# Layer 0's modulation in a two-layer transformer kernel: a third of it on TensorE, two thirds as row products on VectorE

## The reference, cut to what matters

```python
cond_x = jax.nn.silu(c);  cond_c = jax.nn.silu(c_ctx)
for i in range(DEPTH):
    mx = jnp.split((cond_x @ mod_w[i] + mod_b[i])[:, None, :], 6, axis=-1)
    mc = jnp.split(cond_c @ mod_w[i] + mod_b[i], 6, axis=-1)
    hx = x * (1.0 + mx[1]) + mx[0];  hc = ctx * (1.0 + mc[1]) + mc[0]
    yx, yc = mixer(hx, hc)                 # layer 0: HGRN2 with 8 heads, layer 1: window attention
    x = layer_norm(ALPHA * x + mx[2] * yx, ...)
    tokens = x * (1.0 + mx[4]) + mx[3]     # ctx likewise in layer 0
    x = layer_norm(ALPHA * x + mx[5] * peer_ffn(tokens, ...), ...)
```

## Time and profile before

| what | us |
|---|---|
| median of 3 runs (lowest, highest) | 3223.73 (3221.99, 3224.60) |
| the profiled execution: its own time | 3223.5 |
| its span, first to last instruction | 3221.7 |
| TensorE busy in the span | 2920.9 |
| VectorE busy | 2096.4 |
| ScalarE busy | 1157.4 |
| GpSimd busy | 638.0 |

### The profile page before, as it was taken

One profiled execution on the slowest core, in us unless ns is written; L12 is line 12 of the kernel. 1 busy time (PEld: TensorE's weight loads), 2 busy tenths in 40 slices (PEclk: granted clock), 3 DMA queues, 4 the chain that ended last, 5 costly groups with the idle time before them and its releaser, 6 DMA issues.

```text
span 3221.7 us, 43391 instructions
## 1 busy us (share of the span) xinstructions
PE 2920.9 (91%) x15541; PEld 2422.6 (75%) x15541; DVE 2096.4 (65%) x3641; ACT 1157.4 (36%) x1915; POOL 638.0 (20%) x423
## 2 busy tenths in 40 slices
PE   7799996798688999999999999688798789999997
PEld 1488884482377899999999999665597679999997
DVE  0166663479995677777777777845398655656666
ACT  0233330221274333333333333215246544444443
POOL 0000000230343233333333333200464100000000
PEclk9899997899899999999999999899899999999999
DMA  6311102324478888787788878520345766665654
GB/s 260 154 66 65 65 26 79 131 79 157 160 210 275 290 275 280 272 281 274 271 279 274 282 270 283 207 104 27 131 163 174 235 232 211 211 211 209 212 205 147
DMA packets 223271, 623.16 MB, mean 193 GB/s; under 512 B 16296, under 2 KB 104528, under 8 KB 216912
## 3 DMA queue, kind: packets, MB, share of 16 engines
q1 hardware_dynamic: 186332, 487.99, 43.2%
q0 software_dynamic: 36864, 134.23, 12.5%
HBM read 570.68 MB, written 51.48 MB: 193 GB/s over the span
## 4 chain that ended last, share of the span: by engine, by line
PE 78%; DVE 12%; DMA 4%; ACT 2%; POOL 2%; issue 2%; SPq 0%; DVEq 0%; POOLq 0%; ACTq 0%
PE bank L960 28%; PE bank L1005 26%; PE bank L776 5%; PE bank L995 3%; PE bank L883 3%; PE bank L917 2%; PE bank L830 2%; PE bank L741 2%; POOL arena L1934 2%; DVE arena L1727 1%; DMA arena<-in_wst 1%; PE bank L789 1%; DMA arena<-in_u 1%; PE bank L1043 1%; PE bank L1097 1%
## 5 line engine op out<-in xcount | busy, mean ns | idle before, releaser
L960 PE MATMUL bank<-h_parts,u_hi 128*128 128x384 f32 (+1 forms) x3904 | 869.0, 313 | 24.8 <-DVE u_lo L1732 19.9
L1005 PE MATMUL bank<-v_parts,p_hi 128*128 128x512 f32 x2560 | 799.5, 393 | 15.8 <-DVE p_lo L1753 15.4
L960 PEld LDWEIGHTS bank<-h_parts,u_hi 128*128 128x128 f32 x3904 | 676.0, 192 | 44.8 <-issue 17.3
L960 PE MATMUL bank<-h_parts,u_lo 128*128 128x384 f32 (+1 forms) x1952 | 610.4, 313 | 0.0
L1005 PEld LDWEIGHTS bank<-v_parts,p_hi 128*128 128x128 f32 x2560 | 473.2, 189 | 110.7 <-DVE p_lo L1753 14.2
L1005 PE MATMUL bank<-v_parts,p_lo 128*128 128x512 f32 x1280 | 502.4, 393 | 0.0
L1749 DVE TENSOR_TENSOR arena<-arena 128x384 f32<-128x384 f32 (+1 forms) x256 | 190.6, 744 | 418.2 <-ACT arena L1353 392.2
L1353 ACT ACTIVATE arena<-bank 128x384 f32<-128x384 f32 (+1 forms) x232 | 102.8, 443 | 878.1 <-PE bank L960 878.1
L960 PEld LDWEIGHTS bank<-h_parts,u_lo 128*128 128x128 f32 x1952 | 373.8, 192 | 0.0
L1751 DVE TENSOR_TENSOR v_parts<-arena,v_parts 128x1024 fp32r<-128x1024 f32 x256 | 313.7, 1225 | 56.1 <-ACT v_parts L1356 49.3
L1732 DVE TENSOR_TENSOR u_lo<-arena,u_hi 128x1024 fp32r<-128x1024 f32 x230 | 281.2, 1223 | 102.4 <-ACT u_hi L1254 97.8
(11 more groups left out here) (257 smaller groups left out, 3683.5 us busy)
## 6 DMA issues: line engine op xcount, KB each, us to landing
arena<-in_u SPq DMA_DIRECT2D x256, 512.0 KB, 3.6
arena<-in_v SPq DMA_DIRECT2D x256, 512.0 KB, 3.6
arena<-in_wst SPq DMA_DIRECT2D x39, 2048.0 KB, 7.6
gate_scratch<-arena SPq DMA_DIRECT2D x18, 2048.0 KB, 8.7
arena<-gate_scratch SPq DMA_DIRECT2D x32, 768.0 KB
arena<-in_whd SPq DMA_DIRECT2D x8, 2560.0 KB, 9.1
arena<-gate_scratch SPq DMA_DIRECT2D x32, 512.0 KB
x_scratch<-arena SPq DMA_DIRECT2D x10, 512.0 KB, 3.2
```

What stands on the lines that cost most here:

```text
L960: last = mm(banks[q][:, 0:ND[p]], w[:, q, col], h[:, k, DS[p]], start=(n3 == 0), stop=(n3 == 3 * KT - 1))
L1005: last = mm(banks[2 + 2 * b + half][:, :], x[:, q, b * P:(b + 1) * P], y[:, q, col], start=(first and i == 0), stop=(final and i == 2))
```

## The change

1. **Opening.** Only the first four tiles of layer 0's matrix (pieces 0 and 1) go through TensorE. They have four buffers of their own (`mod_at`), so that SP issues all four loads, those of `x` and `ctx` and that of the first head's weights without waiting for a use; each tile's rows are turned right after the next tile's products. The bias is turned into columns and copied to `modcol` first, and the columns of the products are added to it. `x` and `ctx` are loaded into slot `W[1]`; so the second head's weights are loaded once `x` is turned. ScalarE makes the first high parts (`high_w`) behind `modulate_x` and no longer ahead of it, and VectorE the low parts of pieces 0 and 1 behind its low parts of the tokens.
2. **Heads.** The other two thirds of the matrix come transposed (`wm`: 32 blocks of 128x1024, 512 KB, four per head, into two buffers that lie in the area of `hT`). The two conditions go through DRAM and are spread over all partitions (`cb`). For each block and stream VectorE forms the product with the condition and its sum over 1024 elements (`mod_sum`, a `tensor_tensor_reduce`): eight per head, one ahead of level 0, three right after level 0's copy, and one after each of the levels 1, 3, 5 and 7. At a head's end the eight sums are added to `modcol`.
3. **After the heads.** TensorE turns those columns back into rows (two transposes), ScalarE copies them, SP stores them in `modd` with two DMAs, waits for these, and only then issues the loads of the first norm.
4. **Expert loop of layer 0.** Group 1 is written out, and each of its eight steps issues one of the eight loads of the second norm (`ln_row`) behind the step's tile of `v`.
5. The per-slot semaphores of the query weights (`qw_h`, `qw_l`, `qw_pe`) become one each, with waits for the same events. `h_tok` takes scales to which 1 has been added already.

```diff
@@ SP, opening
-            with sp.Fori(0, MOD_TILES // 2) as n:
-                for s in range(2):
-                    sp.wait_ge(mod_pe[s], 1 + n)
-                    sp.dma_start(ar(W[s], KT * WCOLS), a["wst"][2 * n + s]).then_inc(w_loaded[s], 16)
...
-            sp.dma_start(modd[:, 0:MODN], modsb[:, :]).then_inc(mod_out, 16)
+            for i in range(FIRST):
+                sp.dma_start(ar(mod_at[i], KT * WCOLS), a["wst"][i]).then_inc(mod_in[i], 16)
+                if i == 0:
+                    sp.dma_start(lvlraw, a["lvlmask"]).then_inc(lvlmask_in, 16)
             for b in range(2):
                 sp.dma_start(xtok[:, b, :], a["ctx"][0, b * P:b * P + P, :]).then_inc(x_in, 16)
                 sp.dma_start(xtok[:, 2 + b, :], a["x"][0, b * P:b * P + P, :]).then_inc(x_in, 16)
+            sp.dma_start(ar(W[0], WSLOT), a["whd"][0]).then_inc(w_loaded[0], 16)
+            sp.wait_ge(setup_v, 3)
+            sp.dma_start(cs.rearrange("s (k d) -> (s k) d", d=P), condrow).then_inc(cs_out, 16)
+            sp.wait_ge(cs_out, 16)
+            sp.wait_ge(setup_t, 2)
+            sp.wait_ge(xT_pe, KT)
+            sp.dma_start(ar(W[1], WSLOT), a["whd"][1]).then_inc(w_loaded[1], 16)
+            sp.wait_ge(hT_l, KT)
+            for s in range(2):
+                sp.dma_start(cb[:, s, :], cs[s, :].partition_broadcast(P)).then_inc(cb_in, 16)
+            def mod_rows(h, s, x):
+                sp.wait_ge(wm_b, BLOCKS_M * h + (x + 1))
+                sp.dma_start(wm[:, x % 2, :], a["wm"][BLOCKS_M * h + x]).then_inc(wm_in[x % 2], 16)
+            with sp.Fori(0, HEADS // 2 - 1) as n:
                 for s in range(2):
+                    for x in range(BLOCKS_M):
+                        mod_rows(2 * n + s, s, x)
+                        if x == 1:
+                            sp.wait_ge(vproj, 4 * n + (2 * s + 1))
+                            sp.dma_start(ar(W[s], WSLOT), a["whd"][2 * n + (s + 2)]).then_inc(w_loaded[s], 16)
@@ SP, expert loop
+                def experts_and_row(j, q, N):
+                    experts(j, q, N)
+                    ln_row((j - 2) % 8)
...
                 if p == 0:
                     sp.wait_ge(mod1_out, 32)
-                ln_rows(p, 1, STREAMS[p], LN_BASE[p], BLOCKS[p], lambda b: xs[b])
-                with sp.Fori(max(nB, 1), GROUPS - 1) as n:
+                    group(1, experts_and_row)
+                else:
+                    ln_rows(p, 1, STREAMS[p], LN_BASE[p], BLOCKS[p], lambda b: xs[b])
+                with sp.Fori(max(nB, 2), GROUPS - 1) as n:
@@ SP, after the heads
-            sp.wait_ge(mod_out, 16)
+            sp.wait_ge(modT_a, 1)
+            for s in range(2):
+                rows = modd[s, 2 * D:CHUNKS * D].rearrange("(x d) -> x d", d=P)
+                sp.dma_start(rows, modT[:, s, :]).then_inc(mod_out, 16)
+            sp.wait_ge(mod_out, 32)
             ln_rows(0, 0, [0, 1], 0, range(4), x_of)
@@ TensorE
+            def mod_turn(i):
+                pe.wait_ge(mod_v, i + 1)
+                for x in range(4 * i, 4 * i + 4):
+                    last = nc.tensor.transpose(banks[6][:, 2 * x:2 * x + 2], modrow[:, x * P:(x + 1) * P], ident[0:2, 0:2])
+                last.then_inc(mod_t, 1)
+            for i in range(FIRST):
+                pe.wait_ge(mod_in[i], 16)
...
+                for k in range(KT):
+                    last = mm(banks[i % 2][0:2, :], cond[:, :, k], w[:, k, :], start=(k == 0), stop=(k == KT - 1))
+                last.then_inc(mod_pe, 1)
+                if i:
+                    mod_turn(i - 1)
+            mod_turn(FIRST - 1)
@@ ScalarE
-            act.wait_ge(w_loaded[0], 16 * (MT + 1))
+            modulate_x(0)
+            act.wait_ge(w_loaded[0], 16)
             for c in range(2):
                 high_w(0, c)
-            modulate_x(0)
@@ VectorE
+            def mod_sum(h, x, s):
+                col = sums[:, 2 * x + s:2 * x + s + 1]
+                if s == 0:
+                    dve.wait_ge(wm_in[x % 2], 32 * h + (16 * (x // 2) + 16))
+                    dve.wait_ge(wm_b, BLOCKS_M * h + (x + 2))
+                else:
+                    dve.wait_ge(wm_a, BLOCKS_M * h + (x + 1))
+                V.tensor_tensor_reduce(wm_out, wm[:, x % 2, :], cb[:, s, :], 1.0, 0.0, ALU.mult, ALU.add, col).then_inc(wm_b if s else wm_a, 1)
@@ VectorE, levels
                 if more:
                     low_w(h + 1, 1 - slot, 1)
+                mod_sum(h, 0, 0)
...
                     if l == 0:
                         V.tensor_copy(at, src).then_inc(lvlcp, 1)
+                        mod_sum(h, 0, 1)
+                        mod_sum(h, 1, 0)
+                        mod_sum(h, 1, 1)
                         continue
...
                         low_w(h + 1, 1 - slot, l // 2 + 1)
+                    if l % 2:
+                        mod_sum(h, 2 + l // 4, (l // 2) % 2)
@@ VectorE, head's end
                 finish(h, slot)
+                dve.wait_ge(wm_b, BLOCKS_M * h + (2 + BLOCKS_M))
+                m = modcol[:, 0, bass.ds(8 * h + 32, 8)]
+                link(V.tensor_tensor(m, sums, m, ALU.add))
...
-            for c in range(2, 5):
+            for c in range(5):
                 low_w(0, 0, c)
             low_w(1, 1, 0)
+            dve.wait_ge(cb_in, 32)
             scale_head(0, 0)
```

More of the change, by code:

```diff
@@ L178, in build @@
         setup_v = sem("setup_vector")
-        mod_pe = [sem(f"mod_product{i}") for i in range(2)]
-        mod_v = [sem(f"mod_biased{i}") for i in range(2)]
+        mod_in = [sem(f"mod_weights_loaded{i}") for i in range(4)]
+        mod_pe = sem("mod_products")
+        mod_v = sem("mod_rows_copied")
+        cs_out = sem("condition_stored")
+        cb_in = sem("condition_spread")
+        wm_in = [sem(f"mod_rows_loaded{i}") for i in range(2)]
+        wm_a = sem("mod_first_sums")
+        wm_b = sem("mod_sums")
+        modT_a = sem("mod_rows_turned")
         mod_out = sem("mod_stored")
@@ L230, in build @@
         keys_in = sem("keys_loaded")
-        qw_h = [sem(f"query_weights_high{i}") for i in range(4)]
-        qw_l = [sem(f"query_weights_low{i}") for i in range(4)]
-        qw_pe = [sem(f"query_products{i}") for i in range(4)]
+        qw_h = sem("query_weights_high")
+        qw_l = sem("query_weights_low")
+        qw_pe = sem("query_products")
         pq_sb = sem("queries_copied")
@@ L359, in wh @@
             return ar(W[slot], WSLOT, k=KT, n=HCOLS)
-        ORDER = ([("loop", i) for i in range(MOD_TILES)] + [("head", i) for i in range(HEADS)]
+        ORDER = ([("head", i) for i in range(HEADS)]
                  + [("wout0", i) for i in range(2)] + [("wq0", i) for i in range(4)] + [("mod1", i) for i in range(MOD_TILES)]
@@ L734, in _ @@
             nc.tensor.transpose(banks[3][:, 0:24], lbraw, ident[0:24, 0:24]).then_inc(setup_t, 1)
+            pe.wait_ge(bias_in, 16)
+            nc.tensor.transpose(banks[4][:, 0:96], biasraw, ident[0:96, 0:96]).then_inc(setup_t, 1)
             pe.wait_ge(setup_v, 1)
-            with pe.Fori(0, MOD_TILES // 2) as n:
-                for s in range(2):
-                    pe.wait_ge(w_loaded[s], 16 * n + 16)
-                    pe.wait_ge(mod_v[s], 1 + n)
-                    for k in range(KT):
-                        last = mm(banks[s][0:2, :], cond[:, :, k], wt(s)[:, k, :], start=(k == 0), stop=(k == KT - 1))
-                    last.then_inc(mod_pe[s], 1)
+            def mod_turn(i):
[5 more added lines that the diff above has]
+                pe.wait_ge(mod_in[i], 16)
+                w = ar(mod_at[i], KT * WCOLS, k=KT, n=WCOLS)
+                if i >= 2:
+                    pe.wait_ge(mod_v, i - 1)
+                for k in range(KT):
[4 more added lines that the diff above has]
+            mod_turn(FIRST - 1)
             def mod_columns(rows, n, bank):
@@ L747, in mod_columns @@
                 last.then_inc(mod_t, 1)
-            for s in range(2):
-                pe.wait_ge(mod_v[s], 1 + MOD_TILES // 2)
-            mod_columns(modsb, CHUNKS * KT, banks[6])
             def transpose_x(layer, need, src):
@@ L885, in mixer_out @@
                     last.then_inc(y_pe, 1)
+            pe.wait_ge(mod_c, 2)
+            for s in range(2):
+                last = nc.tensor.transpose(banks[7][0:32, s * P:(s + 1) * P], modcol[:, 0, 32 + s:96:2], ident)
+            last.then_inc(mod_t, 1)
             for h in range(HEADS):
@@ L891, in _ @@
             pe.wait_ge(onorm, HEADS)
+            pe.wait_ge(modT_a, 1)
             mixer_out("wout0", oT, WOUT_ORDER[0])
@@ L918, in query_unit @@
                             n3 += 1
-                    last.then_inc(qw_pe[m], 1)
+                    last.then_inc(qw_pe, 1)
                 def key_scores(i):
@@ L1445, in _ @@
             V.tensor_copy(lvlmask.rearrange("p l t -> p (l t)"), lvlraw)
-            dve.wait_ge(bias_in, 32)
-            with dve.Fori(0, MOD_TILES // 2) as n:
-                for s in range(2):
-                    dve.wait_ge(mod_pe[s], 1 + n + 1)
```

(9 more changed lines are left out.)

106 lines of the change are left out of this document (64 added, 42 removed).

## The result

Over four runs each, the changed kernel takes 3139.6 us (median; 3138.6 to 3141.6), the kernel before in the same session 3224.2 (3222.0 to 3224.7). The ratio is 0.974, with a 95% interval of 0.9723 to 0.9757: faster. The forecast was 3144.0, its range 3138 to 3159.

The account below looks back on a forecast made before the run. TensorE was taken to carry the chain in heads and expert loop, its products alternating with loads in the opening. Terms -73.2 + 0.7 + 2.7 - 9.7 = -79.5 took 3223.5 to 3144.0 us; range 3138 to 3159.

Parts of the forecast that it names:

- Opening: Before the first head: fewer tiles on TensorE and earlier tokens start projections at 62.3 against 135.53, minus 73.2 us.
- Clock: TensorE before the projections: idle some 4 us after the change as well, so priced at nothing; up to 1.8 us possible.
- Heads: Seven heads covering a next projection: eight sums each fit VectorE's idle gaps, 0.1 us per head, plus 0.7 us.
- R2: Rival in the heads: waits between sums exceed the gaps, 1 us in each of seven heads, 3150.3 us; chance 0.06.
- Last head: Last head, without a projection: three sums of 3.75 us meet 1.07 idle between levels 0 and 1, plus 2.7 us.
- A sum at 1.25: VectorE's sums in the heads: 1.25 us counted for each, with a wait on the sum before.
- R3: Rival in the heads: a sum costs double, 2.3 us, and misses the gaps, giving 3192 us; chance 0.05.
- Row blocks: Loads in the heads: a third block takes 5.2 us in all against 6 us of room, cost nothing.
- R4: Rival in the heads: row blocks queue behind head weights; a landing of 17 gives 3232 us, slower than before; chance 0.02.
- After the heads: Before the first norm: turning, copying and stores delay its loads 4 to 5 us, covered by 25 us, cost nothing.
- Expert loop: Layer 0's expert loop: spread row loads remove 10.2 us of waiting and slow products, 0.5 given back, minus 9.7 us.
- R1: Rival in the expert loop: the stall spreads over eight steps, most of the 10.2 us returns, 3152 us; chance 0.12.

Follow-up runs that it names:

- e4: The kernel after, with each of the 64 sums computed twice, one behind the other: 3207.2 us.
- e2: The kernel before, with only the second norm's eight row loads spread over the second group of experts, one per expert: 3213.4 us against 3222.5.
- e9: The kernel before, with GpSimd's two low parts of layer 0's first u tiles held back until VectorE has written the last block's choices: 3224.5 us against 3222.4.
- the shifted loop: The kernel after, with 45 small VectorE instructions more ahead of its loop over pairs of heads, the loop itself unchanged: 3138.1 us.
- e3: The kernel after, with each of the 64 sums cut from 1024 to 8 elements, so the modulation sums are left out: 3136.2 us.
- e6: The kernel after, with the last head's eight sums placed one before level 0 and one behind each level from 1 to 7: 3137.1 us.
- e1: The kernel after, with the second norm's eight row loads of layer 0 put back in one batch behind the first group of experts: 3149.4 us.

## Why the prediction was right

**Opening: forecast minus 73.2, measured minus 77.2.** The mechanism held at each step: TensorE sets the end, the fourth tile waits for nothing, the 12.50 us for `x` are gone. Mis-sized was the way to the first `modulate_x`, forecast at 47.3, measured at 43.32. 1.9 us of that are the first tile: I took 13.5 and its products began at 11.63. Half of it is its issue, which moved ahead too (3.62, against 4.56) and which I left out; the other half is its landing in 7.87 us instead of 10.21, 2.3 less where I had taken off 1.4 for the masks. Another 1.9 are products and turns, 29.8 us from 11.63 to 41.47 against 31.7. The slow start gives 1.2 of them: the first two tiles took 15.24 us, not the 9.39 + 7.04 of the earlier trace rows. The turns give 0.5, since two of 0.34 stand between the tiles where I had counted three of 0.4; the third runs beside the last copy. The 1.2 are luck of the execution: the same 32 products take 15.24 us here and 15.53 to 16.72 in the nine experiments with this opening. Their first `modulate_x` stands at 43.40 to 44.61, up to 1.3 us later, but the copy of the first head's level 0 at most 0.8 later (e4 apart, whose sum before it is doubled). From the first `modulate_x` to the projections it is 15.05 us, 15.0 forecast.

**Clock: priced at nothing, and nothing came** ahead of the projections (0.50 in 50 to 60 us). But late in the kernel it made a difference: layer 1's first 16 products took 5.41 us, 3.72 before. Windows of these 10 us, the kernel before, then after:

```profile
2107.00:2117.00 10.00, 8.82 (x38) 7.16 (x39) 3.34 (x9) 0.95 (x3) 0.00 (x0) 1.00 0.00 0
```

```profile
2021.00:2031.00 10.00, 9.30 (x34) 7.47 (x34) 2.77 (x7) 0.56 (x2) 0.00 (x0) 0.83 0.00 1
```

The granted clock is 1.00 before and 0.83 after, for the same work behind the same short turns of `x`. That makes 1.7 of the 2.1 us between 86.4 and 84.3. It is not a price of this change, as far as the runs tell: the same products take 5.41 in e2 and e9 as well, which start from the kernel before, and 3.72 in e4, which has the whole change. What decides when the clock rises there, no run here says.

**Heads: plus 0.7, measured plus 0.4**, of which 0.05 are the sums. The levels did not slip: R2 is out. The 0.3 that is left (the first period over a jump is 45.36 us, 45.09 before) was also there with short sums and is gone in the shifted loop (45.06). That it has to do with the jump is my guess.

**Last head: plus 2.7, measured plus 2.6**, and both e3 and e6 take it away.

**A sum at 1.25, measured 1.22** with starts 1.26 and 1.27 apart. R3 is out, and e4 showed its price to be about right, had the rule held.

**Row blocks.** 32 loads landed in 3.3 us in the median (the page, part 6), and no sum waited for one. R4, with its landing of 16, was far off.

**After the heads: 0, measured 0.2.** The cover of 25 us was there.

**Expert loop: minus 9.7, measured minus 10.1** by the lead, minus 9.1 alone (e2), and 9.8 come back when undone (e1). The 0.5 that I gave back did not show: loads of two rows in a step cost nothing either. R1 is out.

**What the sum lacked:** the 2.1 us of the freed copy and about as much given back in layer 1. That they cancel is luck. 77.2 - 0.4 - 2.6 - 0.2 + 2.4 + 10.1 - 2.1 - 0.5 = 83.9, against 83.8 in the spans. The forecast of 79.5 was short by 4.3, and 4.0 of them are the opening.

## What to carry to other kernels

Work that is off the chain is free only gap by gap: list the idle times in order and put each piece where it fits, and look separately at the iteration that lacks the cover (here the last head, 2.6 us). Before adding instructions to a loop, count it in a trace, waits on semaphores included: a loop of 272 stood 6.6 us at each jump back, and the profile says only "issue". Eight batched loads in front of a stream's next tile made it land after 17.8 us and cost about 10; one or two at a time they cost nothing.

## What was not expected of the hardware

- A loop of 272 or 284 VectorE instructions (as the trace records them, waits included) waits some 6.6 us, then 1.5 to 2.5 us again, behind each jump back, and the instruction queue has about ten packets more; one of 230, in either of two places, does not.
- A VectorE copy or TENSOR_SCALAR within SBUF that starts during a GpSimd subtraction of 128x1024 lasts until about its end: 2.38 us against 0.21, and 2.31 against 0.17. Taking such work out of one place can put another instruction into it.
- The first products after an idle stretch vary among programs that are the same up to there: 32 of them take 15.24 to 16.72 us in the opening, and layer 1's first 16 take either 5.3 to 5.4 or 3.72 us.
